# Moving the scatter of the expert ahead from weight halves 4 and 5 to weight halves 10 and 13

## The reference

```
logits = h @ w_router                       # 256 x 8
top_vals, top_idx = top_k(logits, 2)
combine = sum(one_hot(top_idx) * softmax(top_vals))
y = 0
for e in range(8):
    y += combine[:, e] * ((silu(h @ w_gate[e]) * (h @ w_up[e])) @ w_down[e])
x = x + y
```

## Time and profile before

| what | value |
|---|---|
| median of three runs | 1085.92 us |
| the profiled execution's own time | 1086.23 us |
| its span, first to last instruction | 1084.3 us |
| PE busy | 1071.3 us (99%) |
| DVE busy | 833.8 us (77%) |
| ACT busy | 675.7 us (62%) |
| POOL busy | 73.5 us (7%) |
| moved by DMA | 250.19 MB |
| granted PE clock, mean | 0.999 of full |

### The profile page before, as it was taken

How to read it: one execution, slowest core, us unless ns; L and a number is a source line. 1 busy time by engine, 2 the same in 40 slices (tenths; PEclk the granted TensorE clock), 3 DMA queues, 4 the chain that set the end, 5 groups by cost and what they waited for, 6 DMA issues and landing times.

```text
span 1084.3 us, 16776 instructions
## 1 busy us (share of the span) xinstructions
PE 1071.3 (99%) x6443; PEld 918.3 (85%) x6443; DVE 833.8 (77%) x1166; ACT 675.7 (62%) x959; POOL 73.5 (7%) x119
## 2 busy tenths in 40 slices
PE   8999999999999999999999999999999999999997
PEld 6978788889999998979888878888888888888885
DVE  5679776986555656567956888999889898989896
ACT  5676746555344434756755547876767677777764
POOL 5003330000000000000622000000000000000000
PEclk9999999999999999999999999999999999999999
DMA  9552544567456455355354557899999899999992
GB/s 279 172 192 92 172 139 155 176 233 266 145 178 226 157 165 172 108 181 170 91 191 135 177 158 245 296 358 317 342 323 379 296 356 326 381 325 351 347 350 109
DMA packets 145653, 250.19 MB, mean 231 GB/s; under 512 B 5198, under 2 KB 104612, under 8 KB 145572
## 3 DMA queue, kind: packets, MB, share of 16 engines
q1 hardware_dynamic: 143504, 246.36, 67.0%
q10 hardware_dynamic: 2068, 2.72, 0.7%
HBM read 248.02 MB, written 1.05 MB: 230 GB/s over the span
## 4 chain that ended last, share of the span: by engine, by line
PE 88%; DVE 6%; DMA 3%; ACT 2%; issue 1%; DVEq 0%; ACTq 0%
PE PS L706 27%; PE PS L1254 10%; PE PS L1255 10%; PE PS L1256 10%; PE PS L1051 6%; PE PS L1053 6%; PE PS L1052 6%; PE PS L811 2%; DMA ring<-in_w_exp_up_dram 2%; PE PS L730 2%; PE PS L912 1%; DVE w_lo L448 1%; DVE m_lo L2009 1%; PE PS L1191 1%; DVE scr L2294 1%
## 5 line engine op out<-in xcount | busy, mean ns | idle before, releaser
L448 DVE TENSOR_TENSOR w_lo<-ring,w_hi 128x1536 fp32r<-128x1536 f32 (+1 forms) x191 | 309.4, 1632 | 96.8 <-ACT w_hi L439 96.2
L439 ACT ACTIVATE w_hi<-ring 128x1536 fp32r<-128x1536 f32 (+1 forms) x192 | 264.5, 1387 | 123.6 <-PE PS L1053 71.8
L1481 ACT ACTIVATE m_hi<-ring 128x512 fp32r<-128x512 f32 (+2 forms) x256 | 157.6, 631 | 126.3 <-PE PS L706 121.9
L2009 DVE TENSOR_TENSOR m_lo<-ring,m_hi 128x512 fp32r<-128x512 f32 (+2 forms) x256 | 182.6, 743 | 57.2 <-ACT m_hi L1481 55.0
L1254 PE MATMUL PS<-w_hi,hTe 128*96 128x384 f32 (+1 forms) x384 | 125.1, 326 | 0.0
L1255 PE MATMUL PS<-w_hi,hTe 128*96 128x384 f32 (+1 forms) x384 | 123.9, 323 | 0.0
L1256 PE MATMUL PS<-w_lo,hTe 128*96 128x384 f32 (+1 forms) x384 | 123.7, 322 | 0.0
L706 PE MATMUL PS<-m_hi,h_hi 128*128 128x512 f32 (+3 forms) x320 | 119.4, 373 | 1.4 <-DVE m_lo L2009 1.4
L706 PE MATMUL PS<-m_hi,h_lo 128*128 128x512 f32 (+3 forms) x320 | 115.1, 360 | 0.0
L706 PE MATMUL PS<-m_lo,h_hi 128*128 128x512 f32 (+3 forms) x320 | 115.0, 359 | 0.0
L1051 PE MATMUL PS<-h_hi,w_hi 128*128 128x256 f32 x352 | 99.9, 284 | 0.0
(11 more groups left out here) (356 smaller groups left out, 2188.6 us busy)
## 6 DMA issues: line engine op xcount, KB each, us to landing
ring<-in_w_in_dram SPq DMA_DIRECT2D x39, 1024.0 KB, 5.1
ring<-in_w_exp_gate_dram SPq DMA_DIRECT2D x24, 1536.0 KB, 7.9
ring<-in_w_exp_up_dram SPq DMA_DIRECT2D x24, 1536.0 KB, 9.8
ring<-in_w_exp_down_dram SPq DMA_DIRECT2D x24, 1536.0 KB, 8.7
ring<-in_w_branch_dram SPq DMA_DIRECT2D x12, 1024.0 KB, 5.1
ring<-in_w_ffn_gate_dram SPq DMA_DIRECT2D x6, 1536.0 KB, 6.7
ring<-in_w_ffn_up_dram SPq DMA_DIRECT2D x6, 1536.0 KB, 7.9
ring<-in_w_ffn_down_dram SPq DMA_DIRECT2D x6, 1536.0 KB, 7.1
```

Source lines behind the costliest of these rows:

```text
L439: act.activation(split_parts(u, j)[0], ring[:, i % NSLOT, w0:w0 + words], ACT.Copy)\
L448: dve.tensor_tensor(lo, ring[:, (j // 2) % NSLOT, w0:w0 + words], hi.bitcast(F32), SUB).then_inc(sem(f"lo_ready{b}"), 1)
L1481: act.activation(hi, raw, ACT.Copy).then_inc(sem("m_hi_ready"), 1)
L2009: dve.tensor_tensor(lo, raw, hi.bitcast(F32), SUB).then_inc(sem("m_lo_ready"), 1)
```

## The change

In every expert, `scatter` 0 leaves the place after half 3 and comes after half 9, and `scatter` 1 leaves the place after half 4 and comes after half 12. No operation is added, removed or resized; PE, ACT and DVE all take their order from the table, and the turns of banks 4 and 5 are counted from it too.

```
-EXPERT_AFTER = {3: [("gu", 0), ("scatter", 0)], 4: [("scatter", 1)], 6: [("tr", 0)], 7: [("gu", 1)], 11: [("tr", 1)], 13: [("gu", 2)],
+EXPERT_AFTER = {3: [("gu", 0)], 6: [("tr", 0)], 7: [("gu", 1)], 9: [("scatter", 0)], 11: [("tr", 1)], 12: [("scatter", 1)], 13: [("gu", 2)],
                 17: [("tr", 2)], 19: [("gu", 3)], 20: [("tr", 3)]}
```

## The result

The changed kernel took 1089.03 us in the median of 13 runs (1088.46 to 1092.69), the kernel before 1086.38 beside it (1085.38 to 1090.33). The ratio is 1.0023 with a 95% interval from 1.0013 to 1.0032, so about 2.5 us slower, and clear of no change.

The account below looks back on a forecast made before the run. PE, busy 99% of the span, was taken as the bound, so only its own gaps count. Terms -3.4 + 3.4 + 1.7 gave +1.7 us, 1087.6 us on the scale of the medians, with an 8 in 10 range of 1085.0 to 1090.0.

Parts of the forecast that it names:

- The wait that goes: Behind half 4 in the seven experts with a scatter, PE's gap for banks 4 and 5 goes: 3.4 us saved.
- The new wait in experts 1 and 3: Behind half 9, the gather right after scatter 0 waits for DVE's additions: 1.7 us each, 3.4 in all.
- The new wait in expert 0: Prepare's last piece, after half 12, waits for hdT_lo to free bank 5, behind weigh on DVE: 1.7 us.
- The loads: PE reaches halves 5 to 9 earlier; weights still arrive, 1.7 us left at half 6 of expert 6: cost nothing.
- what would make it wrong: Any PE wait for w_lo at halves 4 to 9, gather without idle, clock below 1.00, or wait before scatter 1.
- rival 1: New waits stay small, 0.8 us in experts 1 and 3, 0.4 in expert 0: sum -1.4, 1084.5 us; chance 0.12.
- Rival 2: Loads set the pace; the 2.5 us saving in experts 2 and 4 to 7 goes: +4.2, 1090.1 us; chance 0.12.
- Rival 3: PE's clock falls to 1.2 GHz after each of three 1.7 us pauses: +6.3, 1093.9 us; chance 0.02.

Follow-up runs that it names:

- the first experiment: Scatter moved to halves 9 and 12 in experts 2, 4, 5, 6 and 7 only, against the kernel before: 1084.32 us, ratio 0.9983.
- the fastest kernel: Against the kernel before, scatter 1 moved to after half 12 in experts 1 to 7, scatter 0 kept after half 3, expert 0 unchanged: 1083.54 us, ratio 0.9973.

## Why the prediction was right, and what it missed

The forecast was 1087.6 us within 1085.0 to 1090.0; the median came at 1089.03, 1.4 above it and inside. The difference to before was forecast as +1.7 and measured as about +2.5 (1.4 to 3.5). The largest single chance stood on "within 0.2%" (0.51), and by its ratio of 1.0023 the change falls just on the slower side (0.41), with 0.2% inside its interval.

**The wait that goes.** Right, in place and size: 3.4 forecast, 3.5 in the profile. The excess of experts 1 and 6, which hung on late loads, did not come back there; 0.3 us came at half 8 of expert 4, which so stayed at 49.3 us where 48.9 to 49.0 had been forecast. That excess is also one execution's: in others unmoved experts 1, 2 and 6 were 0.2 to 0.6 us longer or shorter than in this one.

**The new wait in experts 1 and 3.** Right: 1.7 each, 1.72 measured, and both halves of the working were tried: one experiment took w_lo 12 out of the way, another the two additions.

**The new wait in expert 0.** Right: 1.7 forecast, 1.6 measured. Without weigh ahead of half 14 it was gone, without the selT copies ahead of w_hi 13 it was still 1.1.

**"The loads", which I cost at nothing.** This is the step that failed. It asked only whether the weights of halves 5 to 9 would be there, found 1.7 us to spare at the tightest place, and stopped. PE at half 8 also needs hdT_lo of tr 0, which stands on DVE behind w_lo of half 9. In expert 0 that had 0.38 us to spare and PE came 1.4 us sooner. Its price is 0.76 us in expert 0, in every profile with prepare moved off halves 3 and 4 (0.76, 0.77, 0.79, 0.79, 0.79 at 9 and 12; 0.32 at 4 and 9), and 0.1 to 0.3 in one more expert of some executions, behind a late load. With these 0.76 and 0.30 the sum is +2.8, and the experts of the profile say +2.85. The sentence under "what would make it wrong" named a wait for w_lo at halves 4 to 9; the wait was there, but for another operand.

**Rivals.** The small waits of rival 1 didn't come by themselves; the floor of 0.8 that I gave them was near what the two experiments reached by force (1.0). Rival 2 was refuted by the first experiment: experts 4 and 5 took 48.9 and 49.0 us with a DMA share of 1.00 or 1.01 at 353 GB/s, and PE had no wait in them. The Trainium skill, DMA: Bandwidth & Descriptors, "Where 436 GB/s comes from", gives about 358 GB/s for the HBM side of one core. The rate over an expert lies just under it, but single slices of ten us in the trace of before reached 380 to 391, so no run here shows it as a ceiling. Rival 3: the granted clock stayed at 1.00 in all stretches with pauses of 1.6 and 1.7 us.

**Left open.** Why a load is late in one execution and not in the next (in experts 1 and 6 in one profile, in 2 or 4 in others) was not tried. Nor was the half microsecond between the spans behind the experts' end.

## What to carry to other kernels

Work moved away from a place takes its cover with it: list everything that the engine needs at the next places, every operand and bank and not only the kind that one is looking at, and set each one's ready time against the new arrival. Where several items share two buffers in turn, what counts is the distance to the item ahead in the same buffer and what stands ahead of the reader in its own queue; here one half between two scatters cost 0.4 us each time, and a gather right behind a scatter 1.7. One half between tr 1 and the scatter or prepare after it cost nothing in experts 1 to 7, and 1.6 in expert 0, where weigh stood ahead of the reader. So the distance alone doesn't tell. The forecast's walk along three queues, with durations from rows, came within 0.1 us of each of the three waits that it looked at, and missed the one that it did not.

## What was not expected of the hardware

A DMA share of 1.00 is no sign that the loads are the bound: the same share stood at 347 to 351 GB/s before and, at 1.00 or 1.01, at 352 to 354 in the faster experts. ACT, which reads the loads, did wait for some of them (1.29 us in expert 1 and 0.60 in expert 6 of the fastest kernel), but PE had no wait there.

A matmul that resumes after a wait takes longer once. One of 512 columns is shown with 0.44 to 0.51 us against 0.39 to 0.40, and the next start comes about 0.3 us after it (889.16 to 889.47 in expert 4 before) and not 0.23 (885.99 to 886.22). So each wait costs about 0.1 us more than the time to its release.
